# Decay maps of a gated delta rule: one fp32 product split into two fp32r products by high and low parts

## The chip, the cores and the metric

The kernel runs on one core of a Trainium2 chip. The metric is the device time of one execution in microseconds (us), as the median over runs. The core has a matrix engine (PE, whose weight loads appear as PEld), a vector engine (DVE), a scalar engine (ACT), a general engine (POOL) and a queue engine that issues the transfers (SP).

## The reference

Two layers of a streaming encoder work on 256 tokens of width 1024. Each layer has a token mixer (a gated delta rule with 4 heads of 128 beside a sliding-window attention) and a channel mixer (a dense SwiGLU in layer 0, eight SwiGLU experts with the two best per token in layer 1). The change sits in the decay of the delta rule. With `g` the log decay per token and head, the reference forms running sums inside a chunk and exponentials of their differences:

```python
g = -jnp.exp(a_log) * jax.nn.softplus(a_a + dt_bias)
g_cum = jnp.cumsum(g, axis=-1)
decay = jnp.exp(jnp.where(incl, g_cum[..., :, None] - g_cum[..., None, :], -jnp.inf))
w = einsum(t_mat, k_beta * jnp.exp(g_cum)[..., None])
k_to_end = k * jnp.exp(g_last[..., None] - g_cum)[..., None]
q_decay = q * jnp.exp(g_cum)[..., None]
```

The kernel uses chunks of 128 tokens (two of them) instead of the reference's 64, which gives the same result for the recurrence.

## The kernel before, in words

Every engine has an instruction order written out by hand, and semaphores tie the orders together. Weights arrive in units of 1 MB in a ring of six buffers; ACT casts each unit to fp32r (`w_hi`, L765 for the mixers, L1052 for the experts), DVE takes the rest (`w_lo`, L1805 and L1969), and PE makes three fp32r products per tile out of the two parts (L1136 to L1138 by channel, L1130 to L1132 by token). So nearly all matmuls are fp32r, and only small ones of the delta rule and the attention are plain fp32.

For each layer the mixer runs in this order on PE: the input projection in blocks of 256 columns, then the decay maps, the attention scores, `k_products`, the inverse of the triangular matrix in six levels (L1424 to L1472, each level interleaved with one block of gate weights), the state update over the two chunks, and the output projections.

The decay maps are sums of `g` over ranges of tokens, made by PE as products of a 0/1 matrix with "g rows". DVE first computes `g` for all tokens and heads (L2026 to L2029, four small instructions of 128x8, each waiting for the one before where it needs it). Then at L2034 it multiplies `g`, spread over the 128 columns of a head, by a 0/1 mask. This gives `g_rows[0]` (mask `incl_blk`) and `g_rows[1]` (mask `after_blk`), each of two blocks of 128x512 fp32, and `grow_s` counts up after each of the two. PE's helper `spread` (L1384, its matmul on L1386) multiplies a 0/1 matrix by both blocks of one set of g rows, into two PSUM banks. It is called three times per layer:

- the **first spread**, `spread(after_blk, g_rows[0], 6)`, right after PE has turned the attention's queries and keys (L1324, L1330). PE waits for `grow_s` ahead of it. The scores of the attention (L1343 and L1349) stand behind it in PE's order. ACT takes the exponential of its banks (L915).
- the **second spread**, two calls with `ones` in level 1 of the inverse, on `g_rows[0]` and `g_rows[1]`, behind the level's first products (L1430). The block of gate weights number 1 stands right behind; its `w_lo` comes from DVE (L1805). ACT takes the exponentials of these four banks too, and PE waits for these before the second half of level 1 (L1467).

On DVE, the row maxima of the attention scores (`row_max`, L2046) stand right behind the g rows; they read the banks of the scores. Further on, DVE copies the attention's low parts (L2068), prepares the inverse (L2101 to L2112), and in layer 0 also multiplies conditioning weights between the levels (L1821, L1823).

Of the kernel before, what the change touches and what calls it, by code (L numbers as in the profile page):

```python
# [8 lines left out]
F32 = mybir.dt.float32  # L9
F32R = mybir.dt.float32r  # L10
BF16 = mybir.dt.bfloat16
I32 = mybir.dt.int32
ALU = mybir.AluOpType
# [3 lines left out]
P = 128  # L17
# [6 lines left out]
def build_program(nc, x, c, positions, ada_w, ada_b, norm_mix_w, norm_ffn_w, w_in, conv_w, a_log,  # L24
# [7 lines left out]
    TB = T // P  # L32
    LEVELS = 7
    KEYS1 = 3 * CHUNK
    H = a_log.shape[1]
# [84 lines left out]
    for s, k in enumerate(split_keys):  # L120
        if k[0] in ("fg", "fu", "fd"):
# [3 lines left out]
            b, n_ffn = (2 - n_ffn) % NS_FFN, n_ffn + 1  # L125
        elif k == ("qkvz", 1, 0):
            b = 2
        elif k == ("mix", L - 1, 1, 1):
            b, last_in[2] = 2, split_keys.index(("wa", L - 1, 1))
        else:  # L130
            b = s % NS_MIX
# [45 lines left out]
    with ctx:  # L177
        def sb(name, shape, dt=F32, where=ctx):
            return where.enter_context(nc.sbuf_tensor(name, shape, dt))
# [4 lines left out]
        ps = [ctx.enter_context(nc.psum_tensor(f"bank{b}", [P, 512], F32)) for b in range(8)]  # L184
# [15 lines left out]
        ones = sb("ones", [P, P])  # L200
        incl_blk = sb("incl_blk", [P, P])
        after_blk = sb("after_blk", [P, P])
# [20 lines left out]
        gb = sb("gb", [P, 6, TB, H])  # L223
# [8 lines left out]
        oa_hi = sb("oa_hi", [P, H, T], F32R, gm)  # L232
# [7 lines left out]
        def wk(at, *shape):  # L240
            n = int(np.prod(shape))
            v = work[:, at:at + n]
            if len(shape) == 2:
                return v.rearrange("p (a b) -> p a b", a=shape[0])
            if len(shape) == 3:
                return v.rearrange("p (a b c) -> p a b c", a=shape[0], b=shape[1])
            return v
# [25 lines left out]
        KB = wk(11008, H, T)  # L273
        EG = wk(12032, H, T)
        ED = wk(13056, H, T)
        g_rows = [wk(12032, TB, 512), wk(11008, TB, 512)]
        LT = wk(14080, TB * H, P)
        AT = wk(15104, TB * H, P)
        U = wk(16128, TB * H, P)
# [60 lines left out]
        w_rs = sb("w_rs", [P, KO, E], F32, ge)  # L340
        rb2 = sb("rb2", [P, E], F32, ge)
        wsc3 = sb("wsc3", [P, KO], F32, ge)
        ge.close()


# [293 lines left out]
        def _(pool):  # L639
# [47 lines left out]
            pool.wait_ge(consts, 1)  # L687
            pool.tensor_copy(ident_b[:], ident[:]).then_inc(consts, 1)
            pool.wait_ge(consts, 3)
            for t in (slot_of, wt_of, next_of):  # L690
                pool.memset(t[:], 0.0)
            pool.memset(tok_c[:], 1.0)
# [434 lines left out]
        def _(pe):  # L1127
# [125 lines left out]
            for l in range(L):  # L1253
# [127 lines left out]
                                ins = pe.matmul(o, a_v[:, 0, :], a_pt[:, h, :], start=True, stop=True)  # L1381
                        ins.then_inc(att_ps, 1)

                def spread(lhsT, rows, banks):  # L1384
                    for tb in range(TB):
                        ins = pe.matmul(ps[banks + tb][:], lhsT, rows[:, tb, :], start=True, stop=True)  # L1386
                    ins.then_inc(maps, 1)

                def k_products(other, banks):
# [3 lines left out]
                                            other[:, h, tokens(tb)], start=True, stop=True)  # L1393
                    ins.then_inc(lat, 1)

                pe.wait_ge(grow_s, 2 * l + 1)
                spread(after_blk[:], g_rows[0], 6)
                pe.wait_ge(att_a, NATT_A * l + 3)
                scores(0)
                scores(1)  # L1400
# [23 lines left out]
                for lev in range(1, LEVELS):  # L1424
# [6 lines left out]
                                            start=True, stop=True)  # L1431
                        ins.then_inc(u_ps, 1)
                    if lev == 1:
                        spread(ones[:], g_rows[0], 2)
                        pe.wait_ge(grow_s, 2 * (l + 1))
                        spread(ones[:], g_rows[1], 6)
                    if lev > 1:
                        for tb in range(TB):
                            for h in range(H):
# [333 lines left out]
        def _(dve):  # L1773
# [7 lines left out]
            def link(ins):  # L1781
                dve.wait_ge(dve_c, mark(ins))

            def f32(t):
                return t.bitcast(F32)

            def wide(ap, shape, axis):

                return ap.unsqueeze(axis).to_broadcast(shape)
# [188 lines left out]
            for l in range(L):  # L1978
# [17 lines left out]
                for j in range(6):  # L1996
# [7 lines left out]
                    for tap in range(CTAPS):  # L2004
                        for t in range(2):
# [10 lines left out]
                            else:  # L2016
# [12 lines left out]
                link(dve.scalar_tensor_tensor(gb[:, 5], gb[:, 2], -1.0,  # L2029
                                              wide(head_rows[:, (2 * L + l) * H:(2 * L + l + 1) * H], [P, TB, H], 1),  # L2030
                                              ALU.mult, ALU.mult))
                for rows, mask in ((g_rows[0], incl_blk), (g_rows[1], after_blk)):
                    for tb in range(TB):
                        ins = dve.tensor_tensor(rows[:, tb, :].rearrange("p (h c) -> p h c", h=H),  # L2034
                                                wide(mask[:], [P, H, P], 1),
                                                wide(gb[:, 5, tb, :], [P, H, P], 2), ALU.mult)
                    ins.then_inc(grow_s, 1)

                def row_max(tb):
# [452 lines left out]
```

## Time and profile before

| what | value |
|---|---|
| median of 3 runs | 1757.19 us (1756.1 to 1757.26) |
| the profiled execution, its own time | 1755.13 us |
| its span, first to last instruction | 1753.3 us |
| mean granted clock of PE | 0.998 |
| busy share of PE, DVE, ACT, POOL | 98%, 83%, 62%, 4% |

The span is 1.83 us shorter than the execution's own time; what lies around it is the start and the end of the program. Busy time of PE is modelled at its ends, so instructions overlap on it; the distance between the starts of neighbouring instructions says more about its pace than their durations.

### The profile page before, as it was taken

What the parts mean: (1) busy time and instruction counts of PE and PEld (TensorE: products, weight loads), DVE (VectorE), ACT (ScalarE), POOL (GpSimd) and SP (SyncE); (2) the same over time, 40 slices, a digit from 0 to 9 for tenths busy, and PEclk for the clock granted to TensorE, in tenths of its full rate; (3) what the DMA queues carried; (4) which work ended last, traced back from release to release, by engine and by line L of the source; (5) the groups of instructions that cost most, each with busy time, mean ns of one, the idle gap of its engine ahead of it and who ended that gap; (6) DMA issues with size and microseconds to landing.
All of it is one profiled execution on the core that took longest, in us unless ns stands there. A gap on an engine that the chain in (4) does not pass through costs nothing.

```text
span 1753.3 us, 26724 instructions
## 1 busy us (share of the span) xinstructions
PE 1711.1 (98%) x10287; PEld 1501.2 (86%) x10290; DVE 1461.1 (83%) x1420; ACT 1086.7 (62%) x953; POOL 72.7 (4%) x131
## 2 busy tenths in 40 slices
PE   7999999999999999999999999999999999999997
PEld 6889999999998889988788888888888888888875
DVE  6978688878868664679998998998899989989998
ACT  4564355333445644567677777777777777777775
POOL 4010000000000100000000000010000000000000
PEclk9999999999999999999999999999999999999999
DMA  9735566988973333469999999999999999999994
GB/s 310 258 132 184 153 230 216 338 314 301 330 243 121 121 92 102 140 225 362 332 374 394 357 388 383 364 388 375 367 395 365 377 393 360 385 387 359 394 392 164
DMA packets 261447, 519.97 MB, mean 297 GB/s; under 512 B 12170, under 2 KB 75892, under 8 KB 261364
## 3 DMA queue, kind: packets, MB, share of 16 engines
q1 hardware_dynamic: 257988, 506.21, 81.0%
q0 software_dynamic: 3376, 12.58, 1.8%
q8 instruction: 60, 0.98, 0.2%
q14 instruction: 23, 0.19, 0.0%
HBM read 510.90 MB, written 7.86 MB: 296 GB/s over the span
## 4 chain that ended last, share of the span: by engine, by line
PE 87%; DVE 9%; ACT 2%; issue 1%; DMA 1%; POOL 0%; SPq 0%; DVEq 0%; ACTq 0%; POOLq 0%
PE bank L1130 17%; PE bank L1132 17%; PE bank L1131 17%; PE bank L1136 9%; PE bank L1138 8%; PE bank L1137 8%; DVE w_lo L1969 2%; DVE w_lo L1805 2%; PE bank L1732 1%; PE bank L1430 1%; PE bank L1467 1%; PE bank L1151 1%; DVE ada_acc L1823 1%; DMA ring<-in_ada_w_dram 1%; ACT w_hi L1052 1%
## 5 line engine op out<-in xcount | busy, mean ns | idle before, releaser
L1969 DVE TENSOR_TENSOR w_lo<-ring,w_hi 128x2048 fp32r<-128x2048 f32 x336 | 764.5, 2290 | 84.2 <-ACT w_hi L1052 82.4
L1052 ACT CAST w_hi<-ring 128x2048 fp32r<-128x2048 f32 x336 | 643.3, 1915 | 124.8 <-PE bank L1132 115.6
L1130 PE MATMUL bank<-w_hi,xg_hi 128*128 128x512 f32 x896 | 353.1, 394 | 2.1 <-DVE w_lo L1969 1.7
L1132 PE MATMUL bank<-w_hi,xg_lo 128*128 128x512 f32 x896 | 349.2, 390 | 0.0
L1131 PE MATMUL bank<-w_lo,xg_hi 128*128 128x512 f32 x896 | 348.8, 389 | 0.0
L1136 PE MATMUL bank<-hT_hi,w_hi 128*128 128x256 f32 x1040 | 297.5, 286 | 5.6 <-DVE w_lo L1805 4.9
L1137 PE MATMUL bank<-hT_lo,w_hi 128*128 128x256 f32 x1040 | 290.4, 279 | 0.0
L1138 PE MATMUL bank<-hT_hi,w_lo 128*128 128x256 f32 x1040 | 290.3, 279 | 0.0
L1805 DVE TENSOR_TENSOR w_lo<-ring,w_hi 128x2048 fp32r<-128x2048 f32 x94 | 214.5, 2290 | 61.7 <-ACT w_hi L765 61.6
L765 ACT CAST w_hi<-ring 128x2048 fp32r<-128x2048 f32 x94 | 179.0, 1908 | 57.6 <-PE bank L1138 57.2
L1136 PEld LDWEIGHTS bank<-hT_hi,w_hi 128*128 128x128 f32 x1040 | 195.6, 188 | 9.8 <-DVE w_lo L1805 4.3
L1130 PEld LDWEIGHTS bank<-w_hi,xg_hi 128*128 128x128 f32 x896 | 168.2, 188 | 40.3 <-issue 4.0
L1132 PEld LDWEIGHTS bank<-w_hi,xg_lo 128*128 128x128 f32 x896 | 168.2, 188 | 35.8
L1137 PEld LDWEIGHTS bank<-hT_lo,w_hi 128*128 128x128 f32 x1040 | 195.6, 188 | 1.9 <-issue 1.9
L1131 PEld LDWEIGHTS bank<-w_lo,xg_hi 128*128 128x128 f32 x896 | 168.4, 188 | 33.6
L1138 PEld LDWEIGHTS bank<-hT_hi,w_lo 128*128 128x128 f32 x1040 | 195.5, 188 | 0.0
L1130 PE MATMUL bank<-w_hi,h_hi 128*128 128x512 f32 x448 | 179.2, 400 | 0.0
L1132 PE MATMUL bank<-w_hi,h_lo 128*128 128x512 f32 x448 | 175.1, 391 | 0.0
L1131 PE MATMUL bank<-w_lo,h_hi 128*128 128x512 f32 x448 | 174.4, 389 | 0.0
L1823 DVE SCALAR_TENSOR_TENSOR ada_acc<-ring,c_silu,ada_acc 128x512 f32<-128x512 f32 x162 | 121.7, 751 | 6.0 <-DMA ring<-in_ada_w_dram 0.6
L1132 PEld LDWEIGHTS bank<-w_hi,h_lo 128*128 128x128 f32 x448 | 84.1, 188 | 18.3
L1131 PEld LDWEIGHTS bank<-w_lo,h_hi 128*128 128x128 f32 x448 | 84.3, 188 | 16.1
(434 smaller groups left out, 2010.6 us busy)
## 6 DMA issues: line engine op xcount, KB each, us to landing
ring<-in_moe_w_gate_dram SPq DMA_DIRECT2D x112, 1024.0 KB, 7.8
ring<-in_moe_w_up_dram SPq DMA_DIRECT2D x112, 1024.0 KB, 7.7
ring<-in_moe_w_down_dram SPq DMA_DIRECT2D x112, 1024.0 KB, 7.5
ring<-in_ada_w_dram SPq DMA_DIRECT2D x48, 1024.0 KB, 6.5
ring<-in_w_in_dram SPq DMA_DIRECT2D x38, 1024.0 KB, 5.7
ring<-in_ffn_w_gate_dram SPq DMA_DIRECT2D x14, 1024.0 KB, 6.8
ring<-in_ffn_w_up_dram SPq DMA_DIRECT2D x14, 1024.0 KB, 6.5
ring<-in_ffn_w_down_dram SPq DMA_DIRECT2D x14, 1024.0 KB, 6.7
```

The costliest lines, as they stand in the source:

```text
L765: act.copy(w_hi[buf][:], ring[:, ring_slot, :]).then_inc(hi_ready, 1)
L1052: act.copy(w_hi[MOE_BUF[p % NS_MOE]][:], ring[:, p % RING, :]).then_inc(hi_ready, 1)
L1130: pe.matmul(o, xh, wh, start=start, stop=False)
L1131: pe.matmul(o, xh, wl, start=False, stop=False)
L1132: return pe.matmul(o, xl, wh, start=False, stop=stop)
L1136: pe.matmul(o, wh, xh, start=start, stop=False, skip_group_check=shared)
L1137: pe.matmul(o, wh, xl, start=False, stop=False, skip_group_check=shared)
L1138: return pe.matmul(o, wl, xh, start=False, stop=stop, skip_group_check=shared)
L1151: ins = pe.matmul(ps[bank][:, 4 * q + c:4 * q + c + 1], ada_acc[:, (NQ * l + q) % 2, c * P:(c + 1) * P], ones[:, 0:1], start=not begun, st ...
L1805: dve.tensor_tensor(w_lo[buf_of[s]][:], ring[:, u % RING, :], f32(w_hi[buf_of[s]][:]), ALU.subtract).then_inc(taken, 1)
L1823: ins = dve.scalar_tensor_tensor(acc, w[:, kk, :], ck, acc, ALU.mult, ALU.add)
L1969: dve.tensor_tensor(w_lo[b][:], ring[:, p % RING, :], f32(w_hi[b][:]), ALU.subtract).then_inc(taken, 1)
```

## The change

Each g row set is now written twice. DVE rounds `g` to fp32r (`g_parts[:, 0]`, the high part) and subtracts that from `g` (`g_parts[:, 1]`, the low part). Each part is multiplied by each mask, so there are eight multiplications of 128x512 per layer in place of four, with fp32r results. The order is: high part with `incl_blk`, low part with `incl_blk`, count up `grow_s`; high part with `after_blk`, low part with `after_blk`, count up. In `spread` each bank gets two fp32r products (high, then low) that add up in PSUM, in place of one fp32 product. The 0/1 matrices get fp32r copies, made by POOL at the start of the program. The high parts lie where the g rows lay; the low parts lie in `oa_hi` and `oa_lo`, which the mixer fills only after the inverse.

```diff
-        g_rows = [wk(12032, TB, 512), wk(11008, TB, 512)]
+        gx = ExitStack()
+        sb("before_maps", [P, 15168], F32, gx)
+        g_both = sb("g_both", [P, 2, TB, 512], F32R, gx)
+        gx.close()
+        g_high = [g_both[:, 1], g_both[:, 0]]
+        g_low = [t[:].rearrange("p h t -> p (h t)").rearrange("p (b n) -> p b n", b=TB) for t in (oa_hi, oa_lo)]
...
+        ones_r = sb("ones_r", [P, P], F32R, ge)
+        after_r = sb("after_r", [P, P], F32R, ge)
+        g_parts = sb("g_parts", [P, 2, TB, H], F32R, ge)
...
             pool.wait_ge(consts, 3)
+            pool.tensor_copy(ones_r[:], ones[:])
+            pool.tensor_copy(after_r[:], after_blk[:]).then_inc(consts, 1)
...
-                def spread(lhsT, rows, banks):
+                def spread(lhsT, n, banks):
                     for tb in range(TB):
-                        ins = pe.matmul(ps[banks + tb][:], lhsT, rows[:, tb, :], start=True, stop=True)
+                        pe.matmul(ps[banks + tb][:], lhsT, g_high[n][:, tb, :], start=True, stop=False)
+                        ins = pe.matmul(ps[banks + tb][:], lhsT, g_low[n][:, tb, :], start=False, stop=True)
                     ins.then_inc(maps, 1)
...
+                pe.wait_ge(consts, 4)
                 pe.wait_ge(grow_s, 2 * l + 1)
-                spread(after_blk[:], g_rows[0], 6)
+                spread(after_r[:], 0, 6)
...
-                        spread(ones[:], g_rows[0], 2)
+                        spread(ones_r[:], 0, 2)
                         pe.wait_ge(grow_s, 2 * (l + 1))
-                        spread(ones[:], g_rows[1], 6)
+                        spread(ones_r[:], 1, 6)
...
-                for rows, mask in ((g_rows[0], incl_blk), (g_rows[1], after_blk)):
-                    for tb in range(TB):
-                        ins = dve.tensor_tensor(rows[:, tb, :].rearrange("p (h c) -> p h c", h=H),
-                                                wide(mask[:], [P, H, P], 1),
-                                                wide(gb[:, 5, tb, :], [P, H, P], 2), ALU.mult)
+                link(dve.tensor_copy(g_parts[:, 0], gb[:, 5]))
+                link(dve.tensor_tensor(g_parts[:, 1], gb[:, 5], f32(g_parts[:, 0]), ALU.subtract))
+                for n, mask in enumerate((incl_blk, after_blk)):
+                    for part, rows in enumerate((g_high[n], g_low[n])):
+                        for tb in range(TB):
+                            ins = dve.tensor_tensor(rows[:, tb, :].rearrange("p (h c) -> p h c", h=H),
+                                                    wide(mask[:], [P, H, P], 1),
+                                                    wide(f32(g_parts[:, part, tb, :]), [P, H, P], 2), ALU.mult)
                     ins.then_inc(grow_s, 1)
```

## Rows read from the trace of the kernel before

**Rows 1.** Page, parts 1 and 4: busy time, and the chain that ended last.
```profile
PE 1711.1 (98%) x10287; PEld 1501.2 (86%) x10290; DVE 1461.1 (83%) x1420; ACT 1086.7 (62%) x953; POOL 72.7 (4%) x131
...
PE 87%; DVE 9%; ACT 2%; issue 1%; DMA 1%; POOL 0%; SPq 0%; DVEq 0%; ACTq 0%; POOLq 0%
```

**Rows 2.** Line L1386, durations in ns (min/median/max), first and last start in us.
```profile
L1386 PE MATMUL bank<-work,ones x16: 592/592/595, 141.2 to 636.7; 128*128 128x512 f32 x16
...
L1386 PE MATMUL bank<-work,after_blk x8: 592/592/697, 102.2 to 596.8; 128*128 128x512 f32 x8
```

**Rows 3.** Chain that ended last, layer 0, first spread: start us, us, what.
```profile
100.64 0.18 DVE gb L2029
...
100.84 1.30 DVE work L2034 x2
...
102.19 1.98 PE bank L1386 x4
```

**Rows 4.** Timeline of PEld, layer 0, first spread: start us, us, what, [idle before].
```profile
102.19 0.30 PEld L1386 LDWEIGHTS bank<-work,after_blk 128*128 128x128 f32 x2 [0.32 <-DVE work L2034]
102.73 0.19 PEld L1386 LDWEIGHTS bank<-work,after_blk 128*128 128x128 f32 x1 [0.24 <-issue]
103.16 0.19 PEld L1386 LDWEIGHTS bank<-work,after_blk 128*128 128x128 f32 x1 [0.24 <-issue]
```

**Rows 5.** Timeline of PE among the experts: fp32r products of 512 columns, three starts apart.
```profile
800.02 0.39 PE L1132 MATMUL bank<-w_hi,h_lo 128*128 128x512 f32 x1
...
800.70 0.39 PE L1132 MATMUL bank<-w_hi,h_lo 128*128 128x512 f32 x1
```

**Rows 6.** Page, part 5: the largest group of DVE, fp32r results.
```profile
L1969 DVE TENSOR_TENSOR w_lo<-ring,w_hi 128x2048 fp32r<-128x2048 f32 x336 | 764.5, 2290 | 84.2 <-ACT w_hi L1052 82.4
```

**Rows 7.** Timeline of DVE, layer 0: the first row maximum behind the g rows.
```profile
105.52 0.69 DVE L2046 TENSOR_REDUCE smax<-bank 128x4 f32<-128x512 f32 x1 [2.17 <-PE bank L1349]
```

**Rows 8.** Chain that ended last, second spread of layer 0.
```profile
141.37 3.44 PE bank L1386 x8
144.80 0.12 PE bank L1136
```

**Rows 9.** Chain that ended last, second spread of layer 1.
```profile
633.84 3.44 PE bank L1386 x8
```

**Rows 10.** Timeline of DVE: `w_lo` of gate block 1, layer 0, then layer 1.
```profile
141.21 2.28 DVE L1805 TENSOR_TENSOR w_lo<-ring,w_hi 128x2048 fp32r<-128x2048 f32 x1
...
631.65 2.29 DVE L1805 TENSOR_TENSOR w_lo<-ring,w_hi 128x2048 fp32r<-128x2048 f32 x1
```

**Rows 11.** Chain that ended last, layer 0: PE starting behind a late `w_lo`.
```profile
123.37 0.14 issue
123.51 0.36 PE bank L1136
```

**Rows 12.** Timeline of POOL at the program's start: a cast of 128x128.
```profile
24.98 0.59 POOL L688 CAST ident_b<-ident 128x128 bf16<-128x128 f32 x1
```

**Rows 13.** Windows of 1 us: busy time by engine (count), then PEclk, DMA share, GB/s.
```profile
35.00:36.00 1.00, 0.92 (x4) 0.40 (x3) 0.89 (x3) 0.55 (x2) 0.00 (x0) 0.58 1.11 351
36.00:37.00 1.00, 1.00 (x4) 0.30 (x2) 1.00 (x1) 1.00 (x4) 0.00 (x0) 0.50 1.20 252
37.00:38.00 1.00, 1.00 (x4) 0.33 (x3) 1.00 (x3) 1.00 (x4) 0.00 (x0) 0.50 0.37 45
38.00:39.00 1.00, 1.00 (x7) 0.91 (x6) 1.00 (x5) 1.00 (x4) 0.00 (x0) 0.71 0.13 15
```

**Rows 14.** Timeline of PE just ahead of these windows.
```profile
33.98 1.02 PE L1151 MATMUL bank<-ones,ada_acc 128*128 128x1 f32 x8 [1.03 <-DVE ada_acc L1823]
```

**Rows 15.** Timeline of PE just ahead of the first spread of layer 0.
```profile
100.64 1.09 PE L1324 MATMUL bank<-ident,work 128*128 128x128 f32 x8 [0.53 <-POOL work L709]
101.67 0.44 PE L1330 MATMUL bank<-ident,work 128*128 128x128 f32 x2
```

**Rows 16.** Waits of DVE, 95 to 145 us: total us, times, longest us.
```profile
DVE ob_lo L2068 <- ACT ob_hi L940: 3.7, 2, 2.6
```

## The prediction

> **What bounds the kernel now.** I read the page first. PE is busy for 98% of the span and carries 87% of the chain that ended last [rows 1], so the question is what the change does to PE's clockwork in the two stretches that it touches, once per layer. DVE, with 83%, is the next engine, and the change gives it more work, so each place where PE waits for DVE counts.
>
> Next I read the line of the changed product. An fp32 product of 512 columns leaves two records: 24 records, 8 of the first spread and 16 of the second, stand for 12 products, 6 in each layer [rows 2]. The loads of such passes start 0.43 us apart (102.73 to 103.16) [rows 4], and the chain agrees: 8 passes take 3.44 us [rows 8, 9], again 0.43 each.
>
> Then I read the chain around the first spread. DVE's last small instruction on g starts at 100.64, its first two mask multiplications at 100.84 take 1.30, and PE starts at 102.19 [rows 3]. PE's own row says that it had been idle for 0.32 us and that DVE released it [rows 4]. So here DVE is already late and PE waits: whatever DVE gets to do ahead of the first `grow_s` lands on the path in full. At the second spread it is the other way round. The chain runs through PE alone, and the spread is followed directly by gate block 1 [rows 8], whose `w_lo` was ready at 141.21 + 2.28 = 143.49 [rows 10]. That is only 1.31 us before 144.80.
>
> **The change part by part.**
>
> *DVE ahead of the first spread.* Two small linked instructions are new. From the start of one such to the next work is 0.20 us (100.64 to 100.84) [rows 3], so 0.40. The two multiplications of the low part come ahead of the first `grow_s` too: 2 x 0.65 = 1.30, by the row of the two that are there. Together 1.70 us, all of it on the path. Bounds: the rows show no such instruction with an fp32r result of 512 columns. The nearest one that writes fp32r takes 2.290 for 2048 columns [rows 6], a quarter of that is 0.57; the nearest slower one of 512 columns takes 0.69 [rows 7]. With 0.18 for a small instruction below and 0.20 above, the delay lies between 1.50 and 1.78. I take 1.70, as shape and inputs are those of the existing rows and only the result type is new.
>
> *The first spread itself.* Four fp32 passes become four fp32r passes (two blocks, high and low). Products of fp32r with 512 columns start 0.227 us apart: 800.02 to 800.70 in three steps [rows 5]. Saved: 4 x (0.43 - 0.227) = 0.81. Bounds for a pass: 0.19, what its weight load takes [rows 4], and 0.43, no gain. I take 0.227, since it is the same type, the same width and the same load per product. Net of the first stretch: 1.70 - 0.81 = 0.89 us later, in each layer.
>
> *What is behind it.* The attention scores wait in PE's order behind the spread and come 0.89 later; ACT's exponentials and the row maxima follow them. DVE also has four multiplications more in all, 0.40 + 4 x 0.65 = 3.00 us before its first row maximum. It was idle for 2.17 there, waiting for PE [rows 7], and PE comes 0.89 later, so 3.06 us of cover stand against 3.00. The cover is just enough, and it costs nothing. Where it were gone, each 0.1 us more on DVE would delay the row maxima by 0.1 us.
>
> *The second spread, layer 1.* Eight passes save 8 x 0.203 = 1.62 us on the chain [rows 9]. The next `w_lo` was ready at 631.65 + 2.29 = 633.94 [rows 10], well before PE asks for it. Net of layer 1: 0.89 - 1.62 = -0.73.
>
> *The second spread, layer 0.* PE would be through at 141.37 + 0.89 + 8 x 0.227 = 144.08. But DVE is busy there with conditioning weights before it gets to `w_lo`, and all of it follows the delayed PE: ready at 143.49 + 0.89 = 144.38. A PE that waits for `w_lo` pays 0.14 until it starts, and its first product is 0.36 in the chain [rows 11] where a running one is 0.12 [rows 8]: 144.38 + 0.14 + 0.24 = 144.76, against 144.80 before. So a new wait of PE for DVE eats nearly all of what the spread saves; net of layer 0: -0.04.
>
> *The rest.* POOL's two casts cost some 0.59 each [rows 12], at about 25 us into the program; PE asks for them at 102, and its new wait on `consts` stands ahead of a wait that ends later anyway. Uncovered they would cost 1.2 us once. The other storage of the low parts adds no wait: `oa_hi` and `oa_lo` are filled after the inverse.
>
> *Sum:* -0.04 - 0.73 = -0.77 us. Against the profiled execution's own 1755.13 that is 1754.4; this execution lies 2.06 below the median of the runs, and against the median 1757.19 the sum gives 1756.4.
>
> A rule that speaks for more: the Trainium skill, page "TensorE: Matmul & The Clock Gate", section "Back-to-back issue gap", gives about 131 ns per 512-column product in a stream of load and product pairs. As an estimate by that figure the saving per pass would be 0.30 in place of 0.20 and the time 1754.9; the trace shows 227 ns for such a stream [rows 5], so the row decides and I give that 1 in 100.
>
> **The rivals.**
>
> *PE's clock falls in the new wait.* PE would stand still for 0.32 + 1.70 = 2.0 us ahead of the first spread, after a stretch with only ten small transposes [rows 15]. The profile has one place where the granted clock goes from 1.00 to 0.50, which is 1.2 GHz: after one-column products with a gap of 1.03 us between them [rows 14]. There four windows show 0.58, 0.50, 0.50, 0.71 [rows 13], a loss of 0.42 + 0.50 + 0.50 + 0.29 = 1.71 us. The same here gives 1758.1 in one layer and 1759.8 in both. For it: the gap is twice as long. Against it: the transposes are 128 columns wide, and dense work stands directly before and behind. The Trainium skill, page "TensorE: Matmul & The Clock Gate", section "HAM oscillation — how this bites in real kernels", says that gaps between groups of products put the clock back to its lower level; [rows 13] agree that it can happen in this kernel.
>
> *DVE sets the pace.* If the row maxima start late and nothing makes it up until the inverse is through, the 3.00 us of DVE land on the path in each layer, and the savings of PE lie beside it: +6.0, 1763.2. It decides as soon as DVE's new work clearly exceeds the 3.06 us of cover and no later idle time takes it. Against it: DVE waits again behind, up to 2.6 us for the attention's output [rows 16].
>
> *The fp32r products are no faster.* At 0.43 per pass the change doesn't do what it says: only the 1.70 per layer is left, +3.4, 1760.6. Against it: [rows 5].
>
> *The wait is hidden.* If something else released PE at the first spread, the delay would vanish and all 2 x 2.43 us be saved: 1752.3. Against it: the 0.32 us that PE already waits for DVE [rows 4].
>
> **How the numbers follow.** Forecast 0.76, clock 0.13, products no faster 0.04, DVE sets the pace 0.04, wait hidden 0.02, faster products 0.01. The predicted time is the likeliest, 1756.4. Its own range, from the bounds of the delay (1.50 to 1.78 per layer) and the runs' spread of about 0.6 about their median, is 1755.3 to 1757.4. The range of 8 in 10 takes in the clock in both layers: 1755.0 to 1759.8. A difference of 0.2%, 3.5 us, is about what a measurement of this kernel can tell from no change. Below 1753.7 lies only the hidden wait, with a bit for what I didn't think of: 0.03. Above 1760.7 lies DVE setting the pace, and part of the products that are no faster: 0.05. The rest, 0.92, is within.
>
> **What would show it.** Right: passes of L1386 about 0.23 apart; PE idle for about 2.0 us ahead of the first spread, released by DVE; the first row maximum behind the g rows with almost no idle time; gate block 1 in layer 0 waiting for `w_lo`, and not in layer 1. Wrong: a granted clock of 0.5 after 104 or 597 us (the first spread), passes at 0.43, multiplications well over 0.65 each, or row maxima that start more than 1 us later than before against their scores.

## The result and the profile after: 1769.6 us, slower by 0.7%

The changed kernel takes 1769.63 us (median of 6 runs, 1765.84 to 1772.98), the kernel before beside it 1757.22 us (6 runs, 1755.83 to 1758.64). The ratio is 1.0069, with a 95% interval of 1.0058 to 1.0080. The forecast was 1756.4 with a range up to 1759.8, so the time lies 10 us above the range. The rival that came true is the clock's, at some four times its price. Three executions in the experiments below, of 2435.60 and 6011.08 us (the split wait) and 2443.48 us (before), stand apart from all the others and are left out of the ratios.

The page of the execution profiled after (span 1767.9 us), part 1 and the clock's row of part 2:

```profile
PE 1720.5 (97%) x10290; PEld 1511.2 (85%) x10290; DVE 1466.2 (83%) x1432; ACT 1086.4 (61%) x953; POOL 73.9 (4%) x133
...
PEclk8989999999999899999999999999999999999999
```

Part 1 is nearly that of [rows 1]: PE is still the bound, and the busy shares tell nothing of what happened. The clock's row gives the hint, an 8 in the third and in the fourteenth slice of 44 us. The first spread of layer 0 lies in the third slice, that of layer 1 in the fourteenth. Windows around them show it (columns as in [rows 13], in windows of other lengths):

```profile
104.00:105.00 1.00, 0.18 (x1) 0.21 (x2) 1.00 (x3) 0.26 (x1) 0.00 (x0) 1.00 1.01 393
105.00:106.00 1.00, 1.00 (x4) 0.59 (x3) 1.00 (x3) 0.00 (x0) 0.00 (x0) 0.68 0.10 35
106.00:108.00 2.00, 2.00 (x7) 1.36 (x7) 1.08 (x2) 1.55 (x3) 0.00 (x0) 0.50 0.03 8
...
122.00:123.00 1.00, 1.00 (x9) 1.00 (x9) 1.00 (x5) 1.00 (x6) 0.00 (x0) 0.79 0.00 0
606.00:607.00 1.00, 1.00 (x6) 0.50 (x5) 1.00 (x3) 0.41 (x1) 0.00 (x0) 1.00 0.09 16
607.00:608.00 1.00, 1.00 (x7) 1.00 (x7) 0.64 (x2) 1.00 (x3) 0.00 (x0) 0.56 0.00 0
624.00:625.00 1.00, 1.00 (x10) 1.00 (x9) 0.96 (x2) 0.00 (x0) 0.00 (x0) 0.91 0.00 0
```

At 105 us a share of 0.68 means 0.64 us at half speed, so the clock fell to 1.2 GHz at 105.36; at 122 us 0.79 means 0.42, so it rose at 122.42. That is 17.06 us at half speed. In layer 1 the same reckoning gives 607.12 to 624.18, again 17.06 us. Here the fall is not in the pause itself: the window 104 to 105, in which PE worked for 0.18 us, still shows 1.00, and the fall comes 0.5 us after PE starts again in layer 0 (104.82) and 1.7 us after in layer 1 (605.38).

The chain that ended last, of the kernel after, through the first spread of layer 1, and the first and last pass of its second spread (start us, us, what):

```profile
602.13 0.18 DVE gb L2041
602.34 0.18 DVE g_parts L2044
602.54 0.18 DVE g_parts L2045
602.74 1.29 DVE g_both L2049 x2
604.03 1.21 DVE oa_hi L2049 x2
605.25 0.14 issue
605.38 0.47 PE bank L1396
605.85 0.23 PE bank L1397
606.09 0.23 PE bank L1396
606.32 0.23 PE bank L1397
606.55 0.23 PE bank L1353
606.78 1.67 PE bank L1359 x8
...
617.46 1.57 PE bank L1359 x4
619.03 0.51 PE bank L1146
...
624.23 0.15 PE bank L1148
...
650.69 0.24 PE bank L1396
...
652.32 0.24 PE bank L1397
```

Against [rows 3] this is the forecast, nearly to the hundredth: from the last small instruction on g to PE's start it takes 605.38 - 602.13 = 3.25 us, before 102.19 - 100.64 = 1.55, so the delay is 1.70; the four passes take 1.17, before 1.98, so 0.81 is saved. What comes next was not in the sum. The attention scores (L1359 with the mask's product L1353) reach from 606.55 to 619.03, 12.5 us. In layer 0 they take 13.0 (106.41 to 119.45 in the same chain). At full clock they take 7.3 us, as the first experiment below shows.

PE's timeline of the kernel after, the same place in layer 0:

```profile
104.82 0.47 PE L1396 MATMUL bank<-g_both,after_r 128*128 128x512 f32 x1 [1.79 <-DVE oa_hi L2049]
...
106.79 2.08 PE L1359 MATMUL bank<-work 64*128 64x128 f32 x8
...
119.38 0.58 PE L1146 MATMUL bank<-hT_hi,w_hi 128*128 128x256 f32 x1
...
153.12 0.36 PE L1146 MATMUL bank<-hT_hi,w_hi 128*128 128x256 f32 x1 [0.41 <-DVE w_lo L1817]
```

PE waits 1.79 us for the second pair of DVE's multiplications. Behind the first spread stand the scores, products on 64 rows and 128 or 192 columns, with six wide products of the mask (L1353, 512 or 384 columns) among them; the first product of the next gate block (L1146) comes at 119.38. The clock rises 3.0 us into that block, in layer 1 5.2 us into it.

**Where the 14.6 us of the two profiled executions lie** (their spans are 1767.9 and 1753.3). The program came to layer 0 0.92 us later, with a lower clock between 20 and 40 us (0.67 in that window, before 0.91), which differs from execution to execution: it is 0.91 in the first experiment's and 0.68 in the second's. In layer 0, DVE's subtraction behind the inverse's first level, L2127, starts at 146.79, before at 137.31: 9.48 later. Without the 0.92 that came in and the 0.89 of the forecast, 7.7 us are left for the clock. Between there and layer 1 some 1.2 is given back, so that layer 1's g comes 8.30 later (602.13 against 593.83 for the transposes at the same place). The inverse's level 1 (L1442, before L1430) then starts at 648.64, before at 631.79: 16.85 later, which is 8.55 more, and without 0.89 7.7 for the clock. The second spread gives back 1.6. The remaining 0.7 of saving lies behind it, and I found no place for it.

The two prices agree with the products' own. In layer 0 the scores take 13.0 - 7.3 = 5.8 us more, some 14 products of the block 0.21 in place of 0.117 us each (1.3), and two passes of the spread 0.43 in place of 0.23 (0.4): 7.5. The medians lie only 12.4 apart, so there the clock cost some (12.4 + 0.8) / 2 = 6.6 us per layer. The six executions reach from 1765.84 to 1772.98; how long the clock stayed low in the five that have no profile is not shown.

It was not this one execution. Two stretches of 17.06 us at half speed lower the mean clock of a span of 1768 us by 17.06 / 1768 = 0.0097. All six executions of the changed kernel show 0.984 to 0.988, those of the kernel before 0.993 to 0.998.

### The profile page after: what moved, and what is told of

Its sections match the earlier page's. It is cut to its first block, busy times and chain, and to the rows that moved or that the text cites. A ratio compares the mean times of both kernels' runs of the same rounds, so it can differ in the third digit from the quotient of the medians.

```text
span 1767.9 us, 26743 instructions
## 1 busy us (share of the span) xinstructions
PE 1720.5 (97%) x10290; PEld 1511.2 (85%) x10290; DVE 1466.2 (83%) x1432; ACT 1086.4 (61%) x953; POOL 73.9 (4%) x133
## 4 chain that ended last, share of the span: by engine, by line
PE 87%; DVE 8%; ACT 2%; issue 1%; DMA 1%; POOL 0%; SPq 0%; DVEq 0%; ACTq 0%; POOLq 0%
PE bank L1140 17%; PE bank L1142 17%; PE bank L1141 17%; PE bank L1146 9%; PE bank L1148 8%; PE bank L1147 8%; DVE w_lo L1981 2%; DVE w_lo L1817 2%; PE bank L1744 1%; PE bank L1442 1%; PE bank L1359 1%; PE bank L1479 1%; PE bank L1161 1%; DVE ada_acc L1835 1%; ACT w_hi L1062 1%
## 5 line engine op out<-in xcount | busy, mean ns | idle before, releaser
L1146 PE MATMUL bank<-hT_hi,w_hi 128*128 128x256 f32 x1040 | 298.5, 287 | 5.7 <-DVE w_lo L1817 4.2
L1146 PEld LDWEIGHTS bank<-hT_hi,w_hi 128*128 128x128 f32 x1040 | 197.4, 190 | 10.3 <-issue 4.0
```

Source lines behind the costliest of these rows:

```text
L1146: pe.matmul(o, wh, xh, start=start, stop=False, skip_group_check=shared)
```

## Experiments

The theory ahead of them: the pause of 1.8 us and the thin work behind it bring the clock down, and that is the whole loss. Its rivals: DVE's added work sets the pace; the shorter products alone bring the clock down; the pause alone is enough, whatever stands behind it. In each comparison the kernel before ran beside the others, at 1756.12 to 1756.18 us.

**The pause filled.** Eight products of 512 columns that nobody reads are put ahead of the wait.

```diff
                 pe.wait_ge(consts, 4)
+                warm(8, 6)
                 pe.wait_ge(grow_s, 2 * l + 1)
```

> The changed kernel, with eight dense bf16 products of 512 columns (some 1.7 us, their results overwritten) on PE ahead of the wait for the g rows. Theory (standing still of some 1.8 to 2.0 us behind ten small transposes lets the clock fall): the granted clock stays at 1.00 from the first spread through the scores in both layers, and the time is that of the forecast, 1756.4, within 1755 to 1758. Rival 1 (the fp32r products are too short to hold the clock): it falls all the same, 1768 to 1772. Rival 2 (DVE's additional work sets the pace): near 1769 whatever the clock does.

Measured: 1755.37 us, ratio 0.9994 (0.9985 to 1.0004), 0.8 below the kernel before. Windows of this kernel (columns as above) over both places, and its timeline of PE:

```profile
100.00:130.00 30.00, 29.28 (x201) 24.27 (x202) 26.24 (x49) 18.98 (x54) 0.44 (x1) 1.00 0.22 71
590.00:630.00 40.00, 39.33 (x275) 33.02 (x275) 32.14 (x56) 25.48 (x64) 3.38 (x3) 1.00 0.19 58
```

```profile
102.02 1.67 PE L1185 MATMUL bank<-lev_mask 128*128 128x512 bf16 x7
...
104.68 0.39 PE L1353 MATMUL bank<-am,ident_b 128*128 128x512 bf16 x1
105.01 1.16 PE L1359 MATMUL bank<-work 64*128 64x128 f32 x8
...
111.95 0.38 PE L1146 MATMUL bank<-hT_hi,w_hi 128*128 128x256 f32 x1
...
144.36 0.35 PE L1146 MATMUL bank<-hT_hi,w_hi 128*128 128x256 f32 x1 [0.42 <-DVE w_lo L1818]
```

Its timeline of DVE, the first row maximum behind the g rows of layer 0:

```profile
106.20 0.69 DVE L2062 TENSOR_REDUCE smax<-bank 128x4 f32<-128x512 f32 x1 [0.19 <-PE bank L1359]
```

The first score of the kernel before, for comparison:

```profile
104.32 1.16 PE L1349 MATMUL bank<-work 64*128 64x128 f32 x8
```

DVE's work and the single-pass products are all there, PE starts the spread only 0.1 us sooner behind the transposes (3.16 us behind their start, in the changed kernel 3.26), and yet the clock stays at 1.00 and the scores take 111.95 - 104.68 = 7.3 us. The whole loss is gone. What is left, -0.8, agrees with the sum of the prediction, -0.77, but its interval reaches from -2.6 to +0.7, so the time alone can't tell it from nothing; that the tenths agree is luck. The trace has the terms themselves: single passes 0.23 apart, 0.19 us of idle time on DVE ahead of the row maximum, and PE waiting 0.42 us for `w_lo` in layer 0. DVE is not the bound, and the shorter products do not bring the clock down by themselves. The filling does two things at once, it takes the pause away and puts wide products ahead of the spread; the products alone and the split wait, below, take the pause away without adding any work.

**The delay alone.** The kernel before, with two small instructions and two multiplications of the low part put ahead of its g rows; their results are not used.

```diff
+                link(dve.tensor_copy(g_parts[:, 0], gb[:, 5]))
+                link(dve.tensor_tensor(g_parts[:, 1], gb[:, 5], f32(g_parts[:, 0]), ALU.subtract))
+                for tb in range(TB):
+                    dve.tensor_tensor(oa_hi[:].rearrange("p h t -> p (h t)").rearrange("p (b n) -> p b n", b=TB)
...
                 for rows, mask in ((g_rows[0], incl_blk), (g_rows[1], after_blk)):
```

> The kernel before, with only DVE's additional work ahead of the first count of grow_s: two small instructions and two multiplications of 128x512, whose results nobody reads. All spreads stay fp32. Theory (the standing still alone lets the clock fall): the clock falls to 0.50 at the first spread in both layers for about as long as in the changed kernel (17 us), and the time is 1769 to 1775, a little above the changed kernel's, since nothing is saved. Rival 1 (the shorter products are the cause): the clock stays at 1.00 and the time is 1757.2 + 2 x 1.7 = 1760.6. Rival 2 (DVE's pace): 1760 to 1763 at full clock.

Measured: 1760.22 us (8 runs, 1758.90 to 1767.70), ratio 1.0031 (1.0019 to 1.0043). Its windows and its timeline of PE:

```profile
100.00:130.00 30.00, 27.60 (x194) 22.99 (x193) 24.27 (x48) 19.98 (x57) 1.47 (x2) 1.00 0.22 67
```

```profile
104.69 1.98 PE L1387 MATMUL bank<-work,after_blk 128*128 128x512 f32 x4 [1.69 <-DVE work L2042]
106.81 1.16 PE L1350 MATMUL bank<-work 64*128 64x128 f32 x8
```

I had expected the fall here, so this was a miss. PE pauses for 1.69 us, 0.1 less than in the changed kernel, and the clock stays up in both layers of the profiled execution; the loss of 4.0 is near the two uncovered delays, 3.4. Six of the eight executions have a mean clock of 0.993 or more. The other two, 1767.70 and 1762.06, have 0.989 and 0.991, so the clock probably fell there too; no profile shows where. Between this kernel and the changed one stands the spread: 1.98 us of fp32 passes behind the pause in place of 1.2. Whether it was that or chance that kept the clock up is asked below.

**The single-pass products without the delay.** The first spread reads rows made straight from g twice, the second time in place of the low part, which this kernel leaves out, and DVE counts after its first two multiplications.

```diff
-                        ins = pe.matmul(ps[banks + tb][:], lhsT, g_low[n][:, tb, :], start=False, stop=True)
+                        low_rows = g_high[n] if banks == 6 and n == 0 else g_low[n]
+                        ins = pe.matmul(ps[banks + tb][:], lhsT, low_rows[:, tb, :], start=False, stop=True)
...
+                g_rows_of(g_high[0], incl_blk, gb[:, 5]).then_inc(grow_s, 1)
```

> The change without its delay: DVE writes the fp32r rows of the first spread straight from g and counts up after two multiplications, as before; the other parts follow. The first spread reads the high rows twice, so it leaves out the low part of g (and its high rows are taken from g itself). Theory: PE waits no longer than before, the clock stays at 1.00, and the time is between 1753.0 (all savings of PE kept: 0.81 and 1.62 in layer 1, 1.74 in layer 0 up to w_lo) and 1756.2 (the row maxima start up to 1.6 us late in each layer, since DVE's cover shrinks). Rival 1 (products too short to hold the clock): it falls at the first spread, 1765 to 1770.

Measured: 1752.38 us, ratio 0.9979 (0.9970 to 0.9988), 3.8 below before.

```profile
100.00:130.00 30.00, 29.12 (x204) 24.49 (x204) 26.99 (x51) 19.77 (x56) 1.26 (x2) 1.00 0.23 71
```

The clock is 1.00 here and in layer 1, and PE waits 0.17 us. The short spread with the scores behind it is harmless without the pause. The saving is what single-pass products are worth when DVE's new work is off the path.

**fp32 in the first spread.** The first spread reads g whole, as before, and the high and low rows are made later; only the second spread is single-pass.

```diff
-                spread(after_r[:], 0, 6)
+                first_spread()
...
+                g_rows_of(g_full, incl_blk, gb[:, 5]).then_inc(grow_s, 1)
```

> The whole computation, with the change in the second spread alone: the first spread stays fp32 on fp32 rows that DVE writes first, as before; the high and low rows with incl_blk are made later, ahead of the attention's low part, where DVE stood idle for 2.6 us. Theory: no new wait of PE ahead of the first spread, clock at 1.00; saved 1.62 in layer 1 and 0.93 in layer 0 (then w_lo is late), so 1757.2 - 2.55 = 1754.6, within 1753.5 to 1757. Rival (fp32r spreads as such let the clock fall): over 1762.

Measured: 1753.20 us, ratio 0.9984 (0.9975 to 0.9993), 3.0 below before. The clock is 1.00 at both places. In layer 0 PE still waits for `w_lo`, as expected:

```profile
143.61 0.36 PE L1147 MATMUL bank<-hT_hi,w_hi 128*128 128x256 f32 x1 [0.41 <-DVE w_lo L1823]
```

From the transposes to the second product of the gate block this trace saves 1.5 us in layer 1 (41.88 in place of 43.41) and 0.8 in layer 0 (43.29 in place of 44.12). That is 2.4 of the 3.0; the rest is within the interval, -4.4 to -1.2.

**Work behind the spread.** The changed kernel, with four products of 512 columns that nobody reads between the first spread and the scores.

```diff
                 spread(after_r[:], 0, 6)
+                warm(4, 3)
```

> The changed kernel with its full wait, and four dense bf16 products of 512 columns (0.85 us, results overwritten) behind the first spread and ahead of the scores, so that PE's dense work between the wait and the scores is again as long as the fp32 spread was. Revised theory (the fall needs both the longer pause and the shorter work behind it; the delay alone let the clock fall in the minority of runs): the clock falls in few runs or none, median 1756.4 + 2 x 0.85 = 1758.1, within 1757 to 1761. Rival (the pause decides alone, and in the delay's own experiment it was chance): it falls in nearly all runs, 1768 to 1773.

Measured: 1759.94 us, ratio 1.0026 (1.0016 to 1.0037). The pause is 1.78 us, unchanged. Its windows:

```profile
105.00:106.00 1.00, 0.93 (x4) 0.67 (x4) 1.00 (x2) 0.00 (x0) 0.00 (x0) 0.93 0.28 105
...
109.00:110.00 1.00, 1.00 (x9) 0.88 (x8) 0.00 (x0) 0.36 (x1) 0.00 (x0) 0.86 0.00 0
110.00:114.00 4.00, 4.00 (x22) 2.69 (x22) 3.15 (x7) 1.32 (x8) 0.00 (x0) 1.00 0.00 0
```

The time is in the expected range, the reason was not as expected: the clock should have fallen in few executions or none, and in the profiled one it fell in both layers. In layer 0 it is low from 105.86 to 109.28, in layer 1 as long, 3.4 us, and then stays at 1.00 while the same scores run. So wide products behind the pause did not hold the clock; what differs from the changed kernel is how soon it came back. The scores do not bring it down from 1.00; they only failed to bring it back up. Two of the eight executions, 1765.12 and 1762.17, have mean clocks of 0.990 and 0.992, so the stretch may have been longer there; no profile shows it. Adding products that nobody reads saved 8.6 us: the changed kernel lies 12.4 above before, this one 3.8.

**A gate block behind the spread.** The changed kernel, with the next gate block moved from behind the scores to directly behind the spread.

```diff
                 spread(after_r[:], 0, 6)
+                two_blocks(("qkvz", l, 7), 3)
...
                 scores(1)
-                two_blocks(("qkvz", l, 7), 3)
```

> The changed kernel with its full wait, and the whole dense projection block (48 products of 256 columns, 5.7 us) moved from behind the scores to ahead of them, directly behind the first spread. It asks why the clock stayed low for 17 us. Theory (the scores' thin products, 64 rows high and 128 or 192 columns wide, don't bring the clock back; dense work does): if the clock falls at all, it is back within some 3.5 to 7 us, during the block, and stays up through the scores. The time is confounded by the scores' delay of 5.7 us (PE then waits some 3 to 4 us per layer for the probabilities): 1762 to 1768. Rival (a fall always lasts about 17 us, whatever PE does): low through the block and part of the scores, 1772 or more.

Measured: 1766.47 us, ratio 1.0060 (1.0044 to 1.0076). At the spread it did what the theory says: the clock is low in layer 0 from 103.2 (0.80 in the first window below) to 106.6 (0.69 in the second), 3.4 us that end inside the block, and in layer 1, with a pause of 1.77 us, not at all. But the block had also covered something where it stood. PE now waits 2.7 us for the softmax's divided probabilities, and the clock falls there, for 6.8 us in both layers:

```profile
102.00:104.00 2.00, 0.35 (x1) 0.38 (x2) 2.00 (x4) 1.10 (x3) 0.00 (x0) 0.80 0.95 369
106.00:107.00 1.00, 1.00 (x8) 1.00 (x8) 0.00 (x0) 1.00 (x3) 0.00 (x0) 0.69 0.00 0
...
120.00:128.00 8.00, 6.33 (x32) 5.97 (x33) 7.79 (x17) 6.67 (x21) 0.00 (x0) 0.57 0.00 1
600.00:618.00 18.00, 15.20 (x100) 12.22 (x98) 10.55 (x24) 8.36 (x26) 0.00 (x0) 1.00 0.18 58
```

A pause moved is not a pause removed.

**A longer delay.** The kernel before, with four added multiplications in place of two, and the fp32 spread.

```diff
...
+                for tb in range(TB):
+                    dve.tensor_tensor(oa_lo[:].rearrange("p h t -> p (h t)").rearrange("p (b n) -> p b n", b=TB)
...
```

> The kernel before with twice the multiplications of the delay-alone experiment ahead of the first count: DVE's rows come 0.40 + 4 x 0.65 = 3.0 us later, all spreads fp32. Theory (a pause long enough lets the clock fall whatever follows): it falls in both layers in nearly all runs, 1757.2 + 6 + 13 = 1772 to 1778. Rival (with the dense fp32 spread behind, the clock holds): 1763.2, within 1761 to 1766.

Measured: 1769.26 us (4 runs, 1765.20 to 1772.36), ratio 1.0066 (1.0048 to 1.0085). Its windows:

```profile
104.00:108.00 4.00, 2.27 (x3) 1.18 (x4) 2.88 (x5) 0.07 (x1) 0.00 (x0) 0.59 0.20 79
116.00:120.00 4.00, 4.00 (x12) 2.47 (x10) 1.86 (x3) 2.74 (x16) 0.00 (x0) 0.50 0.00 0
609.00:614.00 5.00, 3.54 (x6) 1.33 (x6) 2.61 (x5) 0.12 (x1) 0.00 (x0) 0.66 0.14 47
614.00:618.00 4.00, 4.00 (x25) 2.96 (x25) 2.04 (x6) 2.96 (x5) 0.00 (x0) 1.00 0.00 0
```

With a pause of 2.89 us the clock falls though the fp32 passes stand behind it. The time lies below the theory's range and above the rival's, as two of the four executions took 1772 us and two 1765 to 1766. In layer 0 the clock stays low for 20.5 us, through 3.6 us of wide fp32 passes and all the scores, in layer 1 for 3.4. PE's instructions at this place are the same in both layers, so the same pause can go either way.

**Ways out: the gate block's first half in the pause.** Half of that block goes ahead of the wait, half stays behind the scores.

```diff
                 pe.wait_ge(consts, 4)
+                one_block(("qkvz", l, 7), 3, 0)
                 pe.wait_ge(grow_s, 2 * l + 1)
...
-                two_blocks(("qkvz", l, 7), 3)
+                one_block(("qkvz", l, 7), 3, 1)
```

> The changed kernel, the whole computation, with half of the last projection block (24 products of 256 columns, 2.8 us, ready long before) moved from behind the scores into PE's wait for the g rows. Theory (the clock falls where PE has a pause of about 2 us and then little dense work): no pause is left, the clock stays at 1.00; against the forecast 1756.4 some 2.0 us of waiting per layer are filled with work that is needed anyway, while the scores come about 0.8 later than in the forecast: 1752.4 if PE alone counts, up to 1756.4 if the scores' delay reaches PE again through ACT. Rival (DVE or ACT set the pace here): 1757 or more at full clock.

Measured: 1753.38 us, ratio 0.9984 (0.9975 to 0.9993), clock 1.00 at both places. PE has a new wait of 0.8 us for ACT behind the scores, of the kind that the other move brought, only shorter.

**Ways out: the wait split.** DVE counts after the high part too; PE does both high products after the first count and both low ones after the second.

```diff
-                pe.wait_ge(grow_s, 2 * l + 1)
-                spread(after_r[:], 0, 6)
+                pe.wait_ge(grow_s, 3 * l + 1)
+                for tb in range(TB):
+                    pe.matmul(ps[6 + tb][:], after_r[:], g_high[0][:, tb, :], start=True, stop=False)
+                pe.wait_ge(grow_s, 3 * l + 2)
...
```

> The changed kernel with the wait cut in two: the high products of the first spread start when the high rows are there, the low ones when the low rows are. The same work on all engines; PE's one pause of 1.8 to 2.0 us becomes one of 0.7 and one of 0.85, and the end of the spread comes 0.45 earlier. If one long pause is what lets the clock fall: full clock, 1755.5. If the sum of work over the stretch counts (revised theory): it falls as in the changed kernel, in all or most runs, about 1768.5.

Measured: 1754.18 us, ratio 0.9987 (0.9977 to 0.9996). The profile is that of one more execution.

> The split wait once more, for a profile of an undisturbed execution. Two pauses of PE at the first spread, 0.7 and below 0.9 us, granted clock 1.00 there in both layers, passes 0.23 us apart, 1753 to 1755.

That execution took 1753.53 us. Its timeline of PE:

```profile
103.52 0.70 PE L1410 MATMUL bank<-g_both,after_r 128*128 128x512 f32 x2 [0.57 <-DVE g_both L2056]
104.63 0.73 PE L1413 MATMUL bank<-oa_hi,after_r 128*128 128x512 f32 x2 [0.41 <-DVE oa_hi L2056]
105.52 1.16 PE L1359 MATMUL bank<-work 64*128 64x128 f32 x8
```

One pause of 1.79 has become two of 0.57 and 0.41, with no work added. The clock is 1.00 in both layers and the scores run at full rate, so the theory that the sum of work over the stretch counts, which had forecast a fall and 1768.5, did not come true.

**Ways out: split and filled.** The same, with nine products of the gate block between the high and the low products.

```diff
+                block_piece(("qkvz", l, 7), 3, 0, range(0, 3))
                 pe.wait_ge(grow_s, 3 * l + 2)
...
-                two_blocks(("qkvz", l, 7), 3)
+                block_piece(("qkvz", l, 7), 3, 0, range(3, KO))
+                one_block(("qkvz", l, 7), 3, 1)
```

> The split wait, and three of eight steps of half a projection block (9 products, 1.05 us, needed anyway) between the high and the low products. The whole computation. If the rest of PE's wait is what can still be had: PE waits 0.40 longer than in the kernel before and for nothing else, so layer 1 gives 0.40 - 2.43 = -2.0 and layer 0, up to w_lo, some -1.3; 1756.2 - 3.3 = 1752.9, and some 1 us below the split wait alone. Rival (the scores' way through ACT and DVE ends last behind the maps): no faster than the split wait or the block in the gap, 1753.5 to 1755.

Measured: 1752.74 us, ratio 0.9979 (0.9970 to 0.9988).

```profile
103.41 0.71 PE L1419 MATMUL bank<-g_both,after_r 128*128 128x512 f32 x2 [0.57 <-DVE g_both L2067]
...
105.01 0.64 PE L1423 MATMUL bank<-oa_hi,after_r 128*128 128x512 f32 x2
```

The second pause is gone. This version does the whole computation and beats both kernels, before by 3.4 us, and so after, which lies 12.4 above before, by 15.8.

What the runs say together (pauses on PE's own rows in layer 0; low stretches in the profiled execution, layer 0 / layer 1; "none" is a granted clock of 1.00):

| kernel | pause of PE | directly behind it | low stretch at the spread | ratio to before |
|---|---|---|---|---|
| before | 0.08 | fp32 spread, 1.98 | none | 1 |
| after | 1.79 | single-pass spread, 1.2, scores | 17.1 / 17.1 | 1.0069 |
| pause filled | filled | single-pass spread, scores | none | 0.9994 |
| delay alone | 1.69 | fp32 spread, scores | none | 1.0031 |
| longer delay | 2.89 | fp32 spread, scores | 20.5 / 3.4 | 1.0066 |
| products alone | 0.17 | single-pass spread, scores | none | 0.9979 |
| work behind | 1.78 | spread, four products, scores | 3.4 / 3.4 | 1.0026 |
| block behind | 1.78 | spread, gate block | 3.4 / none | 1.0060 |
| fp32 in the first spread | 0.17 | fp32 spread, scores | none | 0.9984 |
| half a block in the pause | filled | single-pass spread, scores | none | 0.9984 |
| wait split | 0.57 and 0.41 | high products, low products | none | 0.9987 |
| split and filled | 0.57 | high products, block, low products | none | 0.9979 |

Where no pause at this place was longer than 0.58 us the clock stayed up, in every profile. With pauses of 1.68 us and more it fell in seven of ten passages (five kernels, two layers each). So the pause is needed, and this is shown. Work behind it did not decide whether the clock fell: it fell with four wide products, a gate block or fp32 passes behind as well. How long it stayed low went with that work for the most part: the long stretches, 17.1 and 20.5 us, run through all the scores, and the four of 3.4 us have wide products or fp32 passes in the spread or directly behind it. The longer delay shows both lengths with the same work, so this is not shown as a rule.

## Why the prediction was wrong, by its steps

- **DVE ahead of the first spread: right.** The small instructions start 0.20 apart and two multiplications with fp32r results take 1.21 to 1.29. The delay is 1.70 in layer 1; in layer 0 the chain has 104.82 - 101.56 = 3.26 from DVE's instruction to PE's start, a delay of 1.71 (forecast 1.70). The 0.32 us that the prediction calls PE's own idle time are those of the weight loads [rows 4]; on PE's products the pause before was 102.19 - (101.67 + 0.44) = 0.08 [rows 3, 15], and with the delay it is the 1.79 above. On the weight loads it is 2.00, as forecast.
- **The first spread: right where the clock was up.** Layer 1's passes are 0.23 apart and save 0.81, as forecast. In layer 0 two of them ran at half clock.
- **The rival of the clock: this step failed.** It had the place, the cause and the tell-tale (a granted clock of 0.5 after 104 or 597 us), with a chance of 0.13 and a price of 1.71 us per layer; the loss was 7.7 in each layer of the profiled execution. Two things were wrong in it. The price was that of the one fall in the trace of before [rows 13], 3.4 us in four windows, taken as if a fall had a fixed length. It has not: 3.4, 6.8, 17.1 and 20.5 us were seen. And the argument that kept the chance small, that dense work stands directly behind, was false for this kernel: four short passes stand there, and then the scores, thin products on 64 rows. The list of instructions behind the pause was at hand and I did not read it for this. The argument would not have sufficed either: with wide products or fp32 passes behind, the clock fell for 3.4 us and more in three of four kernels. The Trainium skill, page "TensorE: Matmul & The Clock Gate", section "HAM oscillation — how this bites in real kernels", warns that idle gaps between groups of products put the clock back to its lower level. The trace now agrees, 0.50 from 105.4 to 122.4. The gaps in the page's example are waits for DMA longer than the 1.79 us here, which were enough in this kernel; the measurement decides.
- **Row maxima behind the g rows: right, but only seen where the clock was up.** In the changed kernel DVE was idle for 1.82 us there, because the scores came at half rate. In the kernel with the pause filled it was idle for 0.19, almost nothing as forecast, and the first row maximum starts 106.20 - 105.01 = 1.19 us behind the first score, before 105.52 - 104.32 = 1.20. So the cover of 3.06 against 3.00 sufficed.
- **The second spread: right.** In layer 1 its eight passes take 652.32 + 0.24 - 650.69 = 1.87 us in the chain against 3.44 in [rows 9], a saving of 1.57 (forecast 1.62), and there is no wait behind it. In layer 0 PE waits for `w_lo`, 0.41 us, as forecast.
- **The sum: right in its terms,** by the trace of the kernel with the pause filled. That kernel's time, -0.8 against -0.77, agrees too, but with an interval of -2.6 to +0.7 it proves little. The prediction's narrow range, 1755.3 to 1757.4, is 0.1 and 0.2 wider than its two terms give.
- **The other rivals.** DVE's pace and products that are no faster are ruled out by that kernel and by the spacing of 0.23; the wait was not hidden, as PE's 1.79 us show. By the Trainium skill, page "TensorE: Matmul & The Clock Gate", section "Back-to-back issue gap", a stream of load and product pairs has about 131 ns per product of 512 columns, which would have saved more. These products start 0.23 us apart, and the measurement decides.

What stays open is what exactly the chip weighs when it lowers and raises the clock. The same pause of 2.89 us brought 20.5 us at the lower level in one layer and 3.4 in the other, and one of 1.78 brought 3.4 us in one layer and none in the other (the block behind). That the pause is the cause of the fall is shown for this kernel, as every way of filling or splitting it removed the loss. That the thin work behind it made the stretch long is argued from the profiles above; how long a pause is safe is not shown.

## What to carry to other kernels

Price a new pause of the bounding engine by what the work behind it loses at the lower clock, not by the pause: 1.8 us of waiting cost 7.7 us in the profiled execution, since the clock stayed at 0.50 through the products behind it. Read PE's instructions for the next 15 us before calling the work dense, and rather take the pause away than put work behind it: that still cost 3.8 us with four wide products. Where new work must go ahead of a semaphore, count it up in parts and let the engine start on the first part: that turned +12.4 us into -2.0, and with a piece of other work between the parts into -3.4.

## What the runs showed of the hardware that was not expected

- Against the end of the pause the fall came at different places: 1.0 us ahead of it with the longer delay (104.72 by its window of 0.59, PE back at 105.73), 0.5 and 1.7 us behind it in the changed kernel.
- The scores, products on 64 rows with 128 or 192 columns and six wide ones of the mask among them, left the clock at 0.50 for 13 us though PE had no gap; it rose 3.0 and 5.2 us into the products of 128 x 256 behind them. The same scores left the clock at 1.00 where it stood at 1.00.
- Wide products do not bring it back at once either: 3.6 us of fp32 passes of 512 columns at 0.50 (105.73 to 109.31, the longer delay) left it there.
- A pause of 1.69 us with 1.98 us of fp32 passes behind it left the clock at 1.00 in both layers of the profiled execution; pauses of 1.78 or 1.79 with 1.2 us of single-pass products behind them let it fall in five of six passages.
